# FFN standing tiles read with a step of two from interleaved storage, at sixteen places by piece

## The chip, the cores and the metric

One core of a Trainium2 chip. The metric is the device time of one execution in microseconds; the runs shown are executions of the same program.

## The reference, cut to what matters

Two blocks of two layers each over 256 rows of 1024 features. Every layer is an FFN, a mixer and another FFN, so there are eight FFNs; each is

```python
def swiglu(h, w_gate, w_up, w_down):
    a = jnp.einsum('bsd,df->bsf', h, w_gate)          # 1024 -> 2816
    u = jnp.einsum('bsd,df->bsf', h, w_up)
    return jnp.einsum('bsf,fd->bsd', jax.nn.silu(a) * u, w_down)   # 2816 -> 1024
```

in fp32. The mixers (attention of several kinds, a state-space scan, gated branches) are not touched by the change.

## The kernel before

**Products in halves.** Each fp32 operand is held as two fp32r tensors, `hi` and `lo`, whose sum it is, and each product is made of three: hi by hi, lo by hi and hi by lo. ScalarE writes `whi` from the loaded weights (`hi`, L1781), VectorE subtracts to get `wlo` (`lo`, L2038), in a few places GpSimd does (L2496).

**Pieces.** `plan()` cuts all weights into pieces of at most 1024 columns by 128 partitions in the order of their use; blocks of two pieces (1024 KB) are loaded by SyncE's queue into three `raw` buffers. A piece goes to `whi[i % 5]` and `wlo[i % 5]`, buffers of 1088 elements (4352 B, 17 x 256 B). `PLACES[i]` gives the element at which it starts there: 16 for the FFN's chunks 1 to 20 and some pieces of the mixers, 0 otherwise. The activations `xT` and `hT` start at the same point of 256 B as `wlo[0]` (`lined`).

**FFN.** `ffn` first makes the hidden features, 128 at a time. Chunk 0 goes through `gemm` and `rows`. Chunks 1 to 20 go through `gemm_w` and `columns` (L1589): the weight tile of 128 gate or up columns stands in TensorE, the 256 columns of `xT` move. A piece has four k-tiles of 128 gate and 128 up columns, so 4 x 2 x 3 = 24 matmuls; a chunk has two pieces, 48 matmuls, and its result is gate and up, one 256-column half of a PSUM bank each. ScalarE and VectorE turn it into `h` and then into the two halves of `hT` (`halve_h`, L1837 and L2130; for chunk 0, after a transpose, `turn_h`, L1810 and L2069).

The second gemm (`down`) goes through `rows` (L1570): a 128-column tile of `hT`, for row half t = 0 or 1, stands, and 512 weight columns move. 22 pieces of one k-tile with 2 x 2 x 3 = 12 matmuls, so 264.

Each matmul loads its own standing tile, and the load for the next one runs beside the current one. TensorE executes its queue in order. Between the FFN's up and down parts nothing stalls; `take` keeps `whi` and `wlo` up to five pieces ahead, and a piece's buffer comes free when the piece five before it is used (`hi` waits for `mm`).

Of the kernel before, what the change touches and what calls it, by code (L numbers as in the profile page):

```python
# [9 lines left out]
F32 = mybir.dt.float32  # L10
F32R = mybir.dt.float32r
ACT = mybir.ActivationFunctionType
# [82 lines left out]
QK1 = [[(n, c, c + 128) for n, c in _Q[4 * i:4 * i + 4]] for i in range(5)]  # L95

COLS = {}


def cols_plan():  # L100
# [69 lines left out]
class Signals:  # L170
    def __init__(self, sems):
        self.sems, self.value, self.sure = sems, {}, False
        self.n = {k: 0 for k in sems}
# [54 lines left out]
class Halves:  # L228


    def __init__(self, name, hi, lo, nk, both=None):
        self.name, self.H, self.L, self.both, self.gen = name, hi, lo, both, 0
        self.ready = [[None, None] for _ in range(nk)]
        self.free = ()


class Job:
# [17 lines left out]
    return 0, 0  # L255


PLACES = [place(key) for key, _, _ in plan()]


def upper(m, i):
# [9 lines left out]
def memory(nc, ctx):  # L271

    m = {}

    def sbuf(name, shape, dt=F32, scope=ctx):
        m[name] = scope.enter_context(nc.sbuf_tensor(name, shape, dt))
        return m[name]

    def lined(name, scope=ctx):

        rest = (at_line - nc.sbuf_base) % LINE // 32 * 32
        if rest:
            scope.enter_context(nc.sbuf_tensor(name + "_rest", [128, rest // 4], F32))

    def halves(name, nk, scope=ctx):
        lined(name, scope)
        m[name] = Halves(name, sbuf(name + "_hi", [128, nk, 256], F32R, scope),
                         sbuf(name + "_lo", [128, nk, 256], F32R, scope), nk)

    def many(name, n, shape, dt=F32, scope=ctx):  # L290
        m[name] = [sbuf(f"{name}{i}", shape, dt, scope) for i in range(n)]

    m["ps"] = [ctx.enter_context(nc.psum_tensor(f"ps{i}", [128, 512], F32)) for i in range(8)]
    many("raw", NRAW, [128, BLOCK])
    many("whi", NHL, [128, PIECE + SLACK], F32R)
    at_line = nc.sbuf_base % LINE
    many("wlo", NHL, [128, PIECE + SLACK], F32R)
    many("x", 2, [128, D])
    sbuf("xn", [128, 2, D])
    sbuf("ident", [128, 128])  # L300
    sbuf("cols", [128, NCOLS])
    sbuf("stat", [128, 512])
    sbuf("phalf", [128, 2])
    lined("xT")
    both = sbuf("xT_both", [128, 2, 8, 256], F32R)
    m["xT"] = Halves("xT", both[:, 0, :, :], both[:, 1, :, :], 8, both)

    def ffn(block):
        with ExitStack() as ph:
            halves("hT" + block, 22, ph)  # L310
            many("h" + block, 3, [128, 2, 256], F32, ph)
            sbuf("row" + block, [128, 256], F32, ph)

    with ExitStack() as b1:
        sbuf("rope1", [128, 2, 64], F32, b1)
        sbuf("causal", [128, 384], F32, b1)
        sbuf("dist", [128, 4, 384], F32, b1)
        ffn("1")
        with ExitStack() as ph:
            sbuf("qk1", [128, 18, 256], F32, ph)  # L320
            sbuf("v1", [128, 2, 1152], F32, ph)
            sbuf("o_dil3", [128, 2, 768], F32, ph)
            sbuf("o_dil", [128, 2, 256], F32, ph)
            halves("oTa", 3, ph)
            halves("oTb", 3, ph)
            many("sm1_", 2, [128, 384], F32, ph)
            many("pr1_", 3, [128, 384], F32, ph)
            many("pt1_", 2, [128, 384], F32, ph)
            with ExitStack() as pm:
                sbuf("lat", [128, 2, 416], F32, pm)  # L330
                sbuf("q_mla", [128, 2, 576], F32, pm)
                sbuf("k_mla", [128, 2, 576], F32, pm)
                sbuf("v_mla", [128, 2, 384], F32, pm)
                halves("cq", 2, pm)
                halves("ckv", 1, pm)
                sbuf("rope_a", [128, 2, 96], F32, pm)
                sbuf("rope_b", [128, 2, 96], F32, pm)
                many("qkT", 2, [96, 512], F32, pm)
            sbuf("g1", [128, 2, 3072], F32, ph)
    many("vr", 2, [128, D])  # L340
    sbuf("strict", [128, 384])
    sbuf("chunk", [128, 384])
    sbuf("rope2", [128, 2, 32])
    sbuf("ends", [128, 384])
    ffn("2")
    with ExitStack() as ph:
        sbuf("oa", [128, 2, 1024], F32, ph)
        sbuf("ob", [128, 2, 1024], F32, ph)
        many("sm2_", 2, [128, 385], F32, ph)
        many("pr2_", 3, [128, 384], F32, ph)  # L350
        many("pt2_", 2, [128, 384], F32, ph)
        sbuf("rw", [128, 272], F32, ph)
        sbuf("g2", [128, 6144], F32, ph)
        with ExitStack() as reg2:
            sbuf("bc", [128, 4, 256], F32, reg2)
            sbuf("xd", [128, 2, 1024], F32, reg2)
            many("sums", 2, [128, 4, 256], F32, reg2)
            many("decay", 2, [128, 4, 384], F32, reg2)
            sbuf("cb", [128, 2, 384], F32, reg2)
            many("conv", 3, [128, 256], F32, reg2)  # L360
            many("rot", 2, [128, 512], F32, reg2)
            many("rot_t", 2, [128, 128], F32, reg2)
            sbuf("dt8", [128, 8, 16], F32, reg2)
        sbuf("qkc", [128, 16, 256], F32, ph)
        sbuf("vc", [128, 2, 1024], F32, ph)
        halves("oT2", 8, ph)
    return m
# [1185 lines left out]
def tensor_program(engine, sg, m, steps, *_):  # L1553
    pe, e, at, mark = Lane(engine), engine, sg.at, sg.mark
    pieces, ident = plan(), m["ident"]

    def rows(i, t, job, lo_there, ready, banks):
        _, w, kts = pieces[i]
        hi, lo = upper(m, i), lower(m, i)
        pe.wait_ge(*at("hi", i))  # L1560
        for f in job.free[t]:
            pe.wait_ge(*at(*f))
        sl = slice(128 * t, 128 * t + 128)
        for n, (xs, ws) in enumerate(((job.H, hi), (job.L, hi), (job.H, lo))):
            if n == 2:
                pe.wait_ge(*at(*lo_there))
            for j, (_, kt, _) in enumerate(kts):
                pe.wait_ge(*at(*ready[j]))
                for bank, c0, c1 in [job.outs[t][b] for b in banks if b < len(job.outs[t])]:
                    made = e.matmul(bank[:, 0:c1 - c0], xs[:, kt, sl], ws[:, j * w + c0:j * w + c1],  # L1570
                                    start=kt == 0 and n == 0, stop=kt == job.nk - 1 and n == 2)
        made.then_inc(*mark("mm", i, t, *(banks if banks == (0,) else ())))

    def columns(i, job, lo_there, ready):
        _, w, kts = pieces[i]
        hi, lo = upper(m, i), lower(m, i)
        pe.wait_ge(*at("hi", i))
        for freed in job.free:
            for f in freed:
                pe.wait_ge(*at(*f))  # L1580
        for n, (ws, xs) in enumerate(((hi, job.H), (hi, job.L), (lo, job.H))):
            if n == 2:
                pe.wait_ge(*at(*lo_there))
            for j, (_, kt, _) in enumerate(kts):
                for there in ready[j]:
                    pe.wait_ge(*at(*there))
                for c, out in enumerate(job.outs):
                    o = j * w + 128 * c
                    made = e.matmul(out, ws[:, o:o + 128], xs[:, kt, :], start=kt == 0 and n == 0 and c % 2 == 0,  # L1589
                                    stop=kt == job.nk - 1 and n == 2, skip_group_check=True)  # L1590
        made.then_inc(*mark("mm", i, 1))

# [175 lines left out]
def scalar_program(engine, sg, m, steps, dram):  # L1768
# [38 lines left out]

    def turn_h(s, c, h, ps, free, hT):
        act.wait_ge(*at("tr", "h", s, c))
        e.activation(hT.H[:, 2 * c:2 * c + 2, :].rearrange("p a b -> p (a b)"), ps[:, :], ACT.Copy  # L1810
                     ).then_inc(*mark("xhi", "h", s, c))

    def halve_o(key, src, there, xt, k, n, xfree):
        act.wait_ge(*at(*there))
# [19 lines left out]

    def halve_h(s, c, h, hT):
        act.wait_ge(*at("gated", s, c, 0))
        e.activation(hT.H[:, c + 1, :], h[:, 0, :], ACT.Copy).then_inc(*mark("xhi", "h", s, c))  # L1837

    def mean_square(en, t, halves, rows, xn_free, ss, ms, r):
        for f in xn_free:  # L1840
# [182 lines left out]
def vector_program(engine, sg, m, steps, *_):  # L2023
# [41 lines left out]

    def turn_h(s, c, h, ps, free, hT):
        dve.wait_ge(*at("xhi", "h", s, c))
        hi = hT.H[:, 2 * c:2 * c + 2, :].rearrange("p a b -> p (a b)")
        e.tensor_tensor(hT.L[:, 2 * c:2 * c + 2, :].rearrange("p a b -> p (a b)"), ps[:, :], hi.bitcast(F32), sub  # L2069
                        ).then_inc(*mark("xlo", "h", s, c))  # L2070

    def mean_square(en, t, halves, rows, xn_free, ss, ms, r):
        dve.wait_ge(*at("sumsq", en, t))
# [53 lines left out]

    def halve_h(s, c, h, hT):
        dve.wait_ge(*at("xhi", "h", s, c))
        e.tensor_tensor(hT.L[:, c + 1, :], h[:, 0, :], hT.H[:, c + 1, :].bitcast(F32), sub  # L2130
                        ).then_inc(*mark("xlo", "h", s, c))

    def halve_o(key, src, there, xt, k, n, xfree):
# [489 lines left out]
```

## Time and profile before

| | us |
|---|---|
| median of 2 runs (2783.07 to 2783.18) | 2783.12 |
| the profiled execution | 2783.81 |
| its span, first to last instruction | 2782.0 |
| TensorE busy in it | 2761.5 |

The page gives the busy time of each engine, slices of the span, the chain of work that ended last and the costliest groups. Matmuls are pipelined, and a matmul's duration in the trace is longer than its distance to the next; for the pace of TensorE one divides the length of a stretch of back-to-back matmuls by their number. PE is the matmul side of TensorE, PEld its weight loads.

### The profile page before, as it was taken

The numbers are of one execution on the slowest core, as the hardware profiler recorded it, in microseconds if no ns is written. First come the engines' busy times: TensorE is split into PE (matmuls) and PEld (weight loads), VectorE is DVE, ScalarE is ACT, GpSimd is POOL, SyncE is SP. The second block draws the span as 40 slices with busy tenths as digits, with TensorE's granted clock in tenths as the row PEclk, the third lists the DMA queues.
The fourth block names the chain that finished last, engine by engine and source line by source line (L and its number), as shares of the span: only waits on it lengthen the run. The fifth ranks groups of instructions, "written<-read, shape, count | busy, mean of one in ns | idle before, by whom it ended". The sixth has DMA issues, their size and how long they took to land.

```text
span 2782.0 us, 44672 instructions
## 1 busy us (share of the span) xinstructions
PE 2761.5 (99%) x18116; PEld 2471.4 (89%) x18116; DVE 1822.0 (65%) x2860; ACT 1464.6 (53%) x2398; POOL 239.3 (9%) x187
## 2 busy tenths in 40 slices
PE   9999999999999999999999999999999999999998
PEld 8989889989989889989888987899899888878997
DVE  6656676646656666656568777765565687787755
ACT  6445555545455655444456566445454566655452
POOL 0010011010010010010014100110100131001100
PEclk9999999999999999999999999999999999999999
DMA  6544445555544345555555444555555554445653
GB/s 247 197 168 163 149 156 191 190 188 192 202 171 149 139 172 205 202 185 203 195 189 182 139 171 153 212 197 197 191 201 191 182 188 152 160 159 184 217 193 125
DMA packets 75068, 504.09 MB, mean 181 GB/s; under 512 B 8784, under 2 KB 10480, under 8 KB 19184
## 3 DMA queue, kind: packets, MB, share of 16 engines
q1 hardware_dynamic: 74576, 501.07, 50.7%
q8 instruction: 144, 2.36, 0.3%
q14 instruction: 60, 0.49, 0.1%
q10 hardware_dynamic: 288, 0.17, 0.0%
HBM read 500.12 MB, written 1.08 MB: 180 GB/s over the span
## 4 chain that ended last, share of the span: by engine, by line
PE 92%; DVE 5%; POOL 2%; ACT 1%; issue 1%; DMA 0%; SPq 0%; DVEq 0%; ACTq 0%
PE ps L1570 45%; PE ps L1589 39%; PE ps L1610 3%; POOL wlo L2496 2%; DVE wlo L2038 1%; DVE conv L2325 1%; PE ps L1705 1%; PE ps L1703 1%; PE ps L1730 1%; ACT whi L1781 0%; ACT conv L1949 0%; PE ps L1720 0%; PE ps L1721 0%; PE ps L1722 0%; DVE ps L2142 0%
## 5 line engine op out<-in xcount | busy, mean ns | idle before, releaser
L1781 ACT ACTIVATE whi<-raw 128x1024 fp32r<-128x1024 f32 (+3 forms) x938 | 975.9, 1043 | 636.8 <-PE ps L1570 428.8
L2038 DVE TENSOR_TENSOR wlo<-raw,whi 128x1024 fp32r<-128x1024 f32 (+2 forms) x894 | 1083.8, 1219 | 257.5 <-ACT whi L1781 256.5
L1589 PE MATMUL ps<-xT_both,whi 128*128 128x256 f32 x6592 | 824.2, 278 | 1.0 <-DVE v_mla L2252 1.0
L1589 PEld LDWEIGHTS ps<-xT_both,whi 128*128 128x128 f32 x6592 | 783.1, 188 | 8.3 <-issue 6.9
L1570 PE MATMUL ps<-whi,xT_both 128*128 128x512 f32 (+2 forms) x2336 | 628.6, 391 | 2.9 <-DVE xT_both L2061 1.6
L1570 PEld LDWEIGHTS ps<-whi,xT_both 128*128 128x128 f32 x2336 | 425.3, 188 | 84.2 <-issue 9.3
L1589 PE MATMUL ps<-xT_both,wlo 128*128 128x256 f32 x3296 | 442.5, 277 | 0.0
L1589 PEld LDWEIGHTS ps<-xT_both,wlo 128*128 128x128 f32 x3296 | 405.8, 188 | 0.0
L1570 PE MATMUL ps<-wlo,xT_both 128*128 128x512 f32 (+2 forms) x1168 | 354.4, 384 | 0.3 <-DVE wlo L2038 0.3
L1570 PEld LDWEIGHTS ps<-wlo,xT_both 128*128 128x128 f32 x1168 | 218.3, 188 | 43.7 <-DVE wlo L2038 1.4
L1570 PE MATMUL ps<-whi,hT_hi 128*128 128x512 f32 x704 | 221.4, 390 | 0.0
L1570 PE MATMUL ps<-whi,hT_lo 128*128 128x512 f32 x704 | 220.7, 389 | 0.0
L1570 PE MATMUL ps<-wlo,hT_hi 128*128 128x512 f32 x704 | 220.7, 389 | 0.0
L2496 POOL TENSOR_TENSOR wlo<-raw,whi 128x1024 fp32r<-128x1024 f32 (+1 forms) x44 | 102.5, 2348 | 1274.9 <-ACT whi L1781 1272.9
L2130 DVE TENSOR_TENSOR hT_lo<-h,hT_hi 128x256 fp32r<-128x256 f32 x160 | 68.1, 426 | 197.3 <-ACT hT_hi L1837 197.3
L1570 PEld LDWEIGHTS ps<-wlo,hT_hi 128*128 128x128 f32 x704 | 132.2, 188 | 27.5
L1570 PEld LDWEIGHTS ps<-whi,hT_lo 128*128 128x128 f32 x704 | 132.2, 188 | 27.3
L1570 PEld LDWEIGHTS ps<-whi,hT_hi 128*128 128x128 f32 x704 | 131.6, 188 | 26.6
L1833 ACT ACTIVATE h<-h 128x256 f32<-128x256 f32 x80 | 33.5, 419 | 141.0 <-DVE h L2121 141.0
L1871 ACT ACTIVATE pt<-ps 128x384 f32<-128x384 f32 x96 | 47.1, 491 | 91.8 <-PE ps L1610 90.9
L1830 ACT ACTIVATE h<-ps 128x256 f32<-128x256 f32 x80 | 30.7, 384 | 100.7 <-PE ps L1589 100.7
L2121 DVE TENSOR_TENSOR h<-ps,row 128x256 f32<-128x256 f32 x80 | 33.9, 424 | 68.1 <-PE ps L1589 68.1
(310 smaller groups left out, 2210.9 us busy)
## 6 DMA issues: line engine op xcount, KB each, us to landing
raw<-in_w SPq DMA_DIRECT2D x435, 1024.0 KB, 4.8
vr<-in_vrows SPq DMA_DIRECT2D x19, 512.0 KB, 6.1
raw<-in_w SPq DMA_DIRECT2D x12, 768.0 KB, 4.3
raw<-in_w SPq DMA_DIRECT2D x10, 896.0 KB, 4.5
sums<-scratch SPq DMA_DIRECT2D x8, 512.0 KB, 4.5
raw<-in_w SPq DMA_DIRECT2D x4, 832.0 KB, 4.5
raw<-in_w SPq DMA_DIRECT2D x4, 576.0 KB, 3.7
raw<-in_w SPq DMA_DIRECT2D x4, 512.0 KB, 6.9
```

Of the source, the lines that this page charges most:

```text
L1570: made = e.matmul(bank[:, 0:c1 - c0], xs[:, kt, sl], ws[:, j * w + c0:j * w + c1], start=kt == 0 and n == 0, stop=kt == job.nk - 1 and n == 2)
L1589: made = e.matmul(out, ws[:, o:o + 128], xs[:, kt, :], start=kt == 0 and n == 0 and c % 2 == 0, stop=kt == job.nk - 1 and n == 2, skip_gro ...
L1610: return e.transpose(out, in_, ident[0:k, 0:k])
L1703: e.matmul(ps[:, 0:128], qT[:, 0:128], kT[:, 0:128], start=True, stop=True)
L1781: e.activation(out, raw, ACT.Copy).then_inc(*mark("hi", i))
L1830: e.activation(h[:, 0, :], bank[:, 0:256], ACT.Silu).then_inc(*mark("silu", s, c, 0))
L1833: e.activation(h[:, 0, :], h[:, 0, :], ACT.Silu).then_inc(*mark("silu", s, c, 0))
L1871: e.activation(q[:, :], ps[:, 0:384], ACT.Copy).then_inc(*mark("pT", *key))
L2038: e.tensor_tensor(out, raw, hi.bitcast(F32), sub).then_inc(*mark("lo", i))
L2121: e.tensor_tensor(h[:, 0, :], bank[:, 0:256], row[:, :], mul).then_inc(*mark("scaled", "gate", s, c))
L2130: e.tensor_tensor(hT.L[:, c + 1, :], h[:, 0, :], hT.H[:, c + 1, :].bitcast(F32), sub).then_inc(*mark("xlo", "h", s, c))
L2496: e.tensor_tensor(out, raw, hi.bitcast(F32), ALU.subtract).then_inc(*mark("lo_p", i))
```

## The change

A chunk's piece, for chunks 1 to 20, is stored interleaved: column x of the gate tile at element 2x, column x of the up tile at 2x + 1 (the host writes the weights so). `columns` reads each standing tile with a step of two. In the same way `hT` holds row half t at elements 2x + t, `rows` reads its standing tile with a step of two, and the instructions that write `hT` write with that step; in `turn_h` there are two of them on each engine for one before. The start of these pieces, and of the second gemm's, within their buffers goes through sixteen values, 4 x (5i mod 16) elements for piece i, in place of 16 and 0. What is computed, the number of matmuls, loads and bytes, the order and the waits stay.

```diff
--- before.py
+++ after.py
@@ -97,6 +97,11 @@
+def woven(key):
+
+    return key[1] == "up" and key[3] > 0
+
+
 def cols_plan():
     out, at = [], 0
     for l in (0, 1):
@@ -228,10 +233,20 @@
 class Halves:
 
 
-    def __init__(self, name, hi, lo, nk, both=None):
+    def __init__(self, name, hi, lo, nk, both=None, woven=False):
         self.name, self.H, self.L, self.both, self.gen = name, hi, lo, both, 0
+        self.woven = woven
         self.ready = [[None, None] for _ in range(nk)]
         self.free = ()
+
+
+def by_tile(a):
+    return a.rearrange("p (t x) -> p t x", t=2)
+
+
+def tiles_of(a):
+
+    return a.rearrange("p (x t) -> p t x", t=2)
 
 
 class Job:
@@ -255,7 +270,8 @@
     return 0, 0
 
 
-PLACES = [place(key) for key, _, _ in plan()]
+PLACES = [(4 * (5 * i % 16),) * 2 if key[1] == "down" or woven(key) else place(key)
+          for i, (key, _, _) in enumerate(plan())]
 
 
 def upper(m, i):
@@ -282,10 +298,10 @@
         if rest:
             scope.enter_context(nc.sbuf_tensor(name + "_rest", [128, rest // 4], F32))
 
-    def halves(name, nk, scope=ctx):
+    def halves(name, nk, scope=ctx, woven=False):
         lined(name, scope)
         m[name] = Halves(name, sbuf(name + "_hi", [128, nk, 256], F32R, scope),
-                         sbuf(name + "_lo", [128, nk, 256], F32R, scope), nk)
+                         sbuf(name + "_lo", [128, nk, 256], F32R, scope), nk, woven=woven)
 
     def many(name, n, shape, dt=F32, scope=ctx):
         m[name] = [sbuf(f"{name}{i}", shape, dt, scope) for i in range(n)]
@@ -307,7 +323,7 @@
 
     def ffn(block):
         with ExitStack() as ph:
-            halves("hT" + block, 22, ph)
+            halves("hT" + block, 22, ph, True)
             many("h" + block, 3, [128, 2, 256], F32, ph)
             sbuf("row" + block, [128, 256], F32, ph)
 
@@ -1560,7 +1576,7 @@
         pe.wait_ge(*at("hi", i))
         for f in job.free[t]:
             pe.wait_ge(*at(*f))
-        sl = slice(128 * t, 128 * t + 128)
+        sl = slice(t, t + 255, 2) if job.xt.woven else slice(128 * t, 128 * t + 128)
         for n, (xs, ws) in enumerate(((job.H, hi), (job.L, hi), (job.H, lo))):
             if n == 2:
                 pe.wait_ge(*at(*lo_there))
@@ -1572,7 +1588,7 @@
         made.then_inc(*mark("mm", i, t, *(banks if banks == (0,) else ())))
 
     def columns(i, job, lo_there, ready):
-        _, w, kts = pieces[i]
+        key, w, kts = pieces[i]
         hi, lo = upper(m, i), lower(m, i)
         pe.wait_ge(*at("hi", i))
         for freed in job.free:
@@ -1585,8 +1601,8 @@
                 for there in ready[j]:
                     pe.wait_ge(*at(*there))
                 for c, out in enumerate(job.outs):
-                    o = j * w + 128 * c
-                    made = e.matmul(out, ws[:, o:o + 128], xs[:, kt, :], start=kt == 0 and n == 0 and c % 2 == 0,
+                    tile = slice(j * w + c, j * w + c + 255, 2) if woven(key) else slice(j * w + 128 * c, j * w + 128 * c + 128)
+                    made = e.matmul(out, ws[:, tile], xs[:, kt, :], start=kt == 0 and n == 0 and c % 2 == 0,
                                     stop=kt == job.nk - 1 and n == 2, skip_group_check=True)
         made.then_inc(*mark("mm", i, 1))
 
@@ -1807,8 +1823,9 @@
 
     def turn_h(s, c, h, ps, free, hT):
         act.wait_ge(*at("tr", "h", s, c))
-        e.activation(hT.H[:, 2 * c:2 * c + 2, :].rearrange("p a b -> p (a b)"), ps[:, :], ACT.Copy
-                     ).then_inc(*mark("xhi", "h", s, c))
+        for j in (0, 1):
+            made = e.activation(tiles_of(hT.H[:, 2 * c + j, :]), by_tile(ps[:, 256 * j:256 * j + 256]), ACT.Copy)
+        made.then_inc(*mark("xhi", "h", s, c))
 
     def halve_o(key, src, there, xt, k, n, xfree):
         act.wait_ge(*at(*there))
@@ -1834,7 +1851,7 @@
 
     def halve_h(s, c, h, hT):
         act.wait_ge(*at("gated", s, c, 0))
-        e.activation(hT.H[:, c + 1, :], h[:, 0, :], ACT.Copy).then_inc(*mark("xhi", "h", s, c))
+        e.activation(tiles_of(hT.H[:, c + 1, :]), by_tile(h[:, 0, :]), ACT.Copy).then_inc(*mark("xhi", "h", s, c))
 
     def mean_square(en, t, halves, rows, xn_free, ss, ms, r):
         for f in xn_free:
@@ -2065,9 +2082,10 @@
 
     def turn_h(s, c, h, ps, free, hT):
         dve.wait_ge(*at("xhi", "h", s, c))
-        hi = hT.H[:, 2 * c:2 * c + 2, :].rearrange("p a b -> p (a b)")
-        e.tensor_tensor(hT.L[:, 2 * c:2 * c + 2, :].rearrange("p a b -> p (a b)"), ps[:, :], hi.bitcast(F32), sub
-                        ).then_inc(*mark("xlo", "h", s, c))
+        for j in (0, 1):
+            made = e.tensor_tensor(tiles_of(hT.L[:, 2 * c + j, :]), by_tile(ps[:, 256 * j:256 * j + 256]),
+                                   tiles_of(hT.H[:, 2 * c + j, :]).bitcast(F32), sub)
+        made.then_inc(*mark("xlo", "h", s, c))
 
     def mean_square(en, t, halves, rows, xn_free, ss, ms, r):
         dve.wait_ge(*at("sumsq", en, t))
@@ -2127,7 +2145,7 @@
 
     def halve_h(s, c, h, hT):
         dve.wait_ge(*at("xhi", "h", s, c))
-        e.tensor_tensor(hT.L[:, c + 1, :], h[:, 0, :], hT.H[:, c + 1, :].bitcast(F32), sub
+        e.tensor_tensor(tiles_of(hT.L[:, c + 1, :]), by_tile(h[:, 0, :]), tiles_of(hT.H[:, c + 1, :]).bitcast(F32), sub
                         ).then_inc(*mark("xlo", "h", s, c))
 
     def halve_o(key, src, there, xt, k, n, xfree):
@@ -2590,11 +2608,15 @@
         dst = wpack[at:at + 128 * used].reshape(128, used)
         at += 128 * used
         for i, off, n in ps:
-            _, width, kts = pieces[i]
+            key, width, kts = pieces[i]
+            first = off
             for idx, kt, ranges in kts:
                 for name, c0, c1 in ranges:
                     dst[:, off:off + c1 - c0] = a[name][idx][128 * kt:128 * kt + 128, c0:c1]
                     off += c1 - c0
+            if woven(key):
+                pairs = dst[:, first:off].reshape(128, len(kts), 2, 128)
+                dst[:, first:off] = pairs.transpose(0, 1, 3, 2).reshape(128, -1)
     cols = _np.zeros((128, NCOLS), _np.float32)
     for name, l, c, n in _COLS:
         v = a[name][l]
```

## Rows read from the trace of the kernel before

**Rows 1.** The page's head: busy us (share of the span) and number of instructions.

```profile
span 2782.0 us, 44672 instructions
PE 2761.5 (99%) x18116; PEld 2471.4 (89%) x18116; DVE 1822.0 (65%) x2860; ACT 1464.6 (53%) x2398; POOL 239.3 (9%) x187
```

**Rows 2.** Groups by form, TensorE: shapes, count, busy us, mean ns, idle before.

```profile
L1589 PE MATMUL ps<-xT_both,whi 128*128 128x256 f32 x6592 | 824.2, 278 | 1.0 <-DVE v_mla L2252 1.0
...
L1589 PE MATMUL ps<-xT_both,wlo 128*128 128x256 f32 x3296 | 442.5, 277 | 0.0
L1570 PE MATMUL ps<-whi,hT_hi 128*128 128x512 f32 x704 | 221.4, 390 | 0.0
...
L1604 PE MATMUL ps<-xT_both,whi 128*16 128x256 f32 x32 | 5.7, 279 | 0.0
```

**Rows 3.** Chain of waits, first and last FFN: start us, us, what, count.

```profile
21.41 5.65 PE ps L1589 x48
...
27.95 103.38 PE ps L1589 x912
131.33 58.51 PE ps L1570 x258
...
2610.58 103.38 PE ps L1589 x912
2713.96 53.08 PE ps L1570 x234
```

**Rows 4.** Windows of the first FFN: length, busy us (count), granted clock, DMA share, GB/s.

```profile
27.80:131.10 103.30, 103.30 (x914) 103.30 (x913) 67.41 (x96) 52.69 (x78) 0.00 (x0) 1.00 0.58 205
131.20:189.60 58.40, 58.40 (x260) 48.34 (x259) 27.01 (x28) 23.75 (x27) 2.76 (x3) 1.00 0.50 176
```

**Rows 5.** Timeline of matmuls with 384 moving columns: start us, us, what.

```profile
264.32 0.85 PE L1570 MATMUL ps<-whi,xT_both 128*128 128x384 f32 x4
265.01 0.51 PE L1570 MATMUL ps<-wlo,xT_both 128*128 128x384 f32 x2
265.36 0.85 PE L1570 MATMUL ps<-whi,xT_both 128*128 128x384 f32 x4
```

**Rows 6.** Timeline of weight loads in a run of transposes.

```profile
1694.87 1.56 PEld L1610 LDWEIGHTS ps<-ident,ob 128*128 128x128 f32 x14
1696.40 0.75 PEld L1570 LDWEIGHTS ps<-whi,xT_both 128*128 128x128 f32 x4
```

**Rows 7.** Chain of waits in the first mixer: the chunks' form at two levels.

```profile
218.04 11.54 PE ps L1589 x96
...
239.42 5.66 PE ps L1589 x48
```

**Rows 8.** Timeline of weight loads before chunk 2: a standing tile read without a step.

```profile
27.23 0.53 PEld L1652 LDWEIGHTS ps<-ident,stat 128*128 128x128 f32 x4
27.68 0.65 PEld L1589 LDWEIGHTS ps<-xT_both,whi 128*128 128x128 f32 x5
```

**Rows 9.** Chain of waits: 24 matmuls of L1604, a 16-column standing tile.

```profile
1434.99 2.81 PE ps L1604 x24
```

**Rows 10.** Groups by form in 27.80 to 131.10: the writers of hT.

```profile
L2130 DVE TENSOR_TENSOR hT_lo<-h,hT_hi 128x256 fp32r<-128x256 f32 x19 | 8.1, 426 | 18.8 <-ACT hT_hi L1837 18.8
...
L1837 ACT ACTIVATE hT_hi<-h 128x256 fp32r<-128x256 f32 x19 | 7.6, 400 | 0.0
L2069 DVE TENSOR_TENSOR hT_lo<-ps,hT_hi 128x512 fp32r<-128x512 f32 x1 | 0.7, 692 | 1.2 <-ACT hT_hi L1810 1.2
L1810 ACT ACTIVATE hT_hi<-ps 128x512 fp32r<-128x512 f32 x1 | 0.6, 598 | 1.2 <-PE ps L1610 1.2
```

**Rows 11.** DMA issues in 27.80 to 189.00: count, KB each, median us to landing.

```profile
raw<-in_w SPq DMA_DIRECT2D x27, 1024.0 KB, 4.8
```


## The prediction

> **What bounds the kernel.** I read the page first. TensorE is busy for 2761.5 us of a span of 2782.0 us, VectorE for 65% and ScalarE for 53% [rows 1]. A busy TensorE is not yet a TensorE at its peak, so the next question is how long it takes for one matmul. The groups by form give the counts: 9888 products with a weight chunk standing and 256 columns of activations moving (L1589), and 3 x 704 = 2112 products of the FFN's second gemm, hT standing and 512 weight columns moving (L1570) [rows 2]. Their mean durations (277 and 389 ns) overlap; the chain of waits gives the true pace, since it merges back-to-back matmuls into one piece with a count. In the first FFN, 912 chunk matmuls take 103.38 us, 113.4 ns each, and 258 of the second gemm take 58.51 us, 226.8 ns each; the last FFN shows the same [rows 3]. The 48 of chunk 1 run at 5.65 / 48 = 117.7 ns. The windows show TensorE busy in every microsecond of both stretches at a granted clock of 1.00, its higher level (2.4 GHz), while VectorE has a third of the first stretch free and ScalarE half [rows 4]. So in the FFNs, which the change touches, the pace of TensorE alone sets the time; every nanosecond off a matmul comes off the end.
>
> Matmuls touched: 8 FFNs x 20 chunks x 48 = 7680 chunk matmuls (7296 at 113.4 ns, 384 at 117.7) and 2112 second-gemm matmuls at 226.8 ns. That is 827.4 + 45.2 + 479.0 = 1351.6 us, almost half of the span. Only they can move.
>
> **What a matmul's time is made of.** Six matmuls of 384 columns take 265.36 - 264.32 = 1.04 us, 173.3 ns each [rows 5]; 512 columns take 226.8. So 128 more columns cost 53.5 ns, 0.418 ns each: one column per cycle of 2.4 GHz. Then 512 columns stream in 213.3 ns and 13.5 ns are excess; 256 stream in 106.7 ns and the excess is 6.7 ns, or 11.0 in chunk 1. The other limit is the weight load, of which there is one for each matmul: in transposes, whose 128 moving columns would need only 53 ns, 14 loads take 1696.40 - 1694.87 = 1.53 us, 109.3 ns each [rows 6], 0.854 ns per standing column. So a chunk matmul has two nearly equal limits, 106.7 and 109.3 ns, and takes 113.4.
>
> Where does the excess come from? Not from the other engines: in the first 912 matmuls ScalarE and VectorE start and stop some 170 times, and the mean is 113.4 ns at both ends of the kernel [rows 3, 4]. But the same form takes 113.4 ns in one stretch and 117.7 or 120.2 ns in another [rows 3, 7], with the same operands and no idle time inside. So part of the excess depends on how the two reads of TensorE itself, the moving tile and the next standing tile, stand to each other. With a step of one the moving read advances 4 B per 0.418 ns (9.6 B/ns) and the standing read 4 B per 0.854 ns (4.7 B/ns): one overtakes the other through whatever banks the storage has, again and again. With a step of two the standing read advances 8 B per 0.854 ns, 9.4 B/ns: the two run side by side and hardly overtake. That is the mechanism I take as likeliest.
>
> **The change, part by part.**
>
> *Chunk matmuls (standing tile read with a step of two).* If the overtaking is the excess, what remains is the load's 109.3 ns: 7296 x (113.4 - 109.3) = 29.9 us and 384 x (117.7 - 109.3) = 3.2 us, together -33 us. Bounds: no change gives 0; a load cannot come under 109.3 by any row, so -33 is also the end of the gain. On the other side a strided load may be dearer. The one standing tile of this trace that is not read contiguously (a step of zero, L1652) takes 27.68 - 27.23 = 0.45 us for four, 112.5 ns [rows 8]; that is the nearest row, and at 112.5 ns the gain shrinks to 7296 x 0.9 + 384 x 5.2 = 8.6 us. I take 109.3, since a step of zero hits one spot of the storage and a step of two does not.
>
> The Trainium skill, "SBUF — State Buffer", Specifications, says storage is read by 16-byte lines that want at least two hits each for full bandwidth. A step of two in fp32 has exactly two hits per line, so by that page the strided load keeps its pace; a step of four would not. No row of the trace of before shows a step of two.
>
> *Second gemm (hT standing with a step of two, weights moving from sixteen places).* The load fits twice into the matmul, so only the stream and its excess count. The smallest excess of any row is 6.7 ns [rows 3]; at 213.3 + 6.7 = 220.0 the gain is 2112 x 6.8 = 14.4 us. Ends: none, and the whole excess, 2112 x 13.5 = 28.5 us. One row speaks for a floor under the excess: with a standing tile of only 16 columns, where hardly any load runs beside the stream, 256 columns still take 2.81 / 24 = 117 ns [rows 2, 9]. I take 14.4.
>
> The Trainium skill, "TensorE: Matmul & The Clock Gate", Back-to-back issue gap, gives N/2.4 + 2.5 ns. By that page 512 columns would take 215.8 ns, and the second term would be 2112 x 11.0 = 23 us instead of 14.4.
>
> *Places.* A piece starts at 4 x (5i mod 16) elements, 16 B steps over 256 B; hT and xT stay where they were. One piece in sixteen has both reads start at the same place. There I price a collision as the slow rows do: a chunk matmul at 117.7 rather than 109.3, 480 x 8.4 = 4.0 us; a second-gemm matmul at 226.8 rather than 220.0, 132 x 6.8 = 0.9 us. So +5 us.
>
> *ScalarE and VectorE.* The two halves of an hT tile are now written with a step of two (L1837, L2130: 400 and 426 ns), and the first tile's halves in two instructions rather than one (598 and 692 ns, once per FFN) [rows 10]. If the strided writes took double, each engine would carry 0.4 us more for each chunk of 5.4 us; VectorE is busy for 67.41 of 103.30 us there. Hidden, zero. Without that cover it would be 160 x 0.4 = 64 us, but nothing in TensorE's queue waits for an hT tile until the second gemm, up to twenty chunks later. Transfers: a block of 1024 KB lands in 4.8 us [rows 11]; two pieces would take 2 x 24 x 0.1093 = 5.25 us, and three blocks are in flight or in use. Hidden, though with less room than before (5.44 us). The host's reordering of the weights costs the device nothing, and bytes and packets are the same.
>
> Sum: -33 - 14 + 5 = -42 us. The profiled execution took 2783.8 us (its span 2782.0 and 1.8 around it), 0.7 above the median; the difference holds for both, so 2783.1 - 42 = **2741 us**, or -1.5%.
>
> **The rivals.**
>
> *Faster still.* All excess of the second gemm goes and no place collides: -33 - 28.5 = -61.6 us, 2721.5. For it: the excess of 13.5 ns is twice that of the chunks, so it is not one constant. Against it: the 16-column row.
>
> *The excess is not made by the two reads* (the change doesn't do what it says). Then it is fixed per matmul and only the 384 slow ones might move: 2780 to 2783. For it: the 16-column row again, and excesses that are the same to 0.1 ns in all eight FFNs. The Trainium skill, "SBUF — State Buffer", Who interferes with whom, says TensorE has two independent read ports and never waits for anyone; by that page this rival is right. The two levels of the same form [rows 3, 7] speak against it.
>
> *Side by side is worse.* Reads that advance at one pace stay wherever they begin; if they begin in a collision they may keep it. If most places behave as the slow rows, 7296 x 4.3 = 31 us and, at the same share (4%) for the second gemm, 19 us are added: 2833.
>
> *The strided load is slow.* This one decides for slower. A chunk matmul has only 113.4 - 109.3 = 4.1 ns of room above its load. With the second gemm's gain of 14 us kept, the kernel is slower as soon as a load with a step of two takes over 113.4 + 1.9 = 115.3 ns, 5% more than a contiguous one; by over 2% from 122.6 ns. At one and a half times the contiguous load, 164 ns, it is 7680 x 50 = +390 us, 3160 us; at twice, +800. Nothing in the trace excludes it, as no row reads so; what speaks against it is that the moving stream takes 9.6 B/ns and a strided load asks for 9.4.
>
> **How the numbers follow.** I give 0.52 to the forecast with its own range 2728 to 2760; 0.08 to faster still; 0.16 to no change (2770 to 2785); 0.11 to side by side is worse (2785 to 2835); 0.13 to the slow load. A measurement of this kernel tells 2% from no change, 55.7 us: under 2727.5 is faster, over 2838.8 slower. Faster gets 0.07, slower 0.14, the same 0.79. The range from 2721 to 2815 holds the forecast, nearly all of faster still, no change and over half of the worse case: about 0.8.
>
> **What the profile after would show.** In the chain of waits the piece of 912 should shrink from 103.4 to about 100 us, and the 258 from 58.5 to about 56.8. Chunk 1 should lose its slow level. If the load is slow, the weight loads of L1589 will be longer than 188 ns and lie end to end. If the places decide, pieces of one FFN will differ with a period of sixteen, where now all are equal. VectorE's idle time before wlo should shrink a little. All else, the mixers above all, should keep its microseconds; if they move, I have missed a coupling.

## The result and the profile after

| | before | after |
|---|---|---|
| median, us | 2783.12 (2783.07 to 2783.18) | 2842.97 (2842.66 to 2843.29) |
| span of the profiled execution, us | 2782.0 | 2841.5 |
| TensorE busy, us | 2761.5 | 2820.5 |

The ratio is 1.0215, with a 95% interval of 1.0171 to 1.0259: 59.9 us slower, by the median a little over the 2% bound, which the interval includes. I had forecast 2741 us and a range up to 2815.

The page's head of the changed kernel (answers to [rows 1]): TensorE's busy time grew by 59.0 us, ScalarE's by 2.8 and VectorE's by 0.1.

```profile
span 2841.5 us, 44688 instructions
PE 2820.5 (99%) x18116; PEld 2534.1 (89%) x18116; DVE 1822.1 (64%) x2868; ACT 1467.4 (52%) x2406; POOL 239.5 (8%) x187
```

The chain of waits of the changed kernel, first and last FFN: start us, us, what, count (answers to [rows 3]).

```profile
22.02 5.74 PE ps L1605 x48
...
28.64 109.35 PE ps L1605 x912
...
137.99 59.88 PE ps L1586 x258
...
2662.82 109.35 PE ps L1605 x912
2772.17 54.31 PE ps L1586 x234
```

912 chunk matmuls take 109.35 us where they took 103.38: 119.9 ns each, not 113.4. 258 of the second gemm take 59.88 where they took 58.51: 232.1 ns, not 226.8. Over eight FFNs that is 8 x 5.97 = 47.8 us, and 2112 x 1.37 / 258 = 11.2 us; chunk 1 (5.74 for 5.65) gives 0.7. Together 59.7 us: the whole difference, and all of it in the matmuls that the change touches.

Groups by form of the changed kernel in 28.5 to 137.8, the first FFN's chunks (the writers of hT answer to [rows 10]), and below them the weight loads of the kernel before in 27.8 to 131.1:

```profile
L1605 PEld LDWEIGHTS ps<-xT_both,whi 128*128 128x128 f32 x608 | 75.7, 196 | 0.0
...
L2148 DVE TENSOR_TENSOR hT_lo<-h,hT_hi 128x256 fp32r<-128x256 f32 x19 | 8.1, 426 | 22.1 <-ACT hT_hi L1854 22.1
...
L1854 ACT ACTIVATE hT_hi<-h 128x256 fp32r<-128x256 f32 x19 | 8.0, 420 | 0.0
```

```profile
L1589 PEld LDWEIGHTS ps<-xT_both,whi 128*128 128x128 f32 x608 | 71.7, 188 | 0.0
```

The record of a weight load is 8 ns longer, as I had written for the slow load. By itself this sign proves little: in the first FFN of `places_even` below, where the tiles are contiguous and the matmuls also take 120.0 ns, the records of the loads are 192 ns. The strided writes cost nothing on VectorE (426 ns in both) and 20 ns on ScalarE, hidden.

### The profile page after: what moved, and what is told of

Same layout as the page of the kernel before. It is cut to its first block, busy times and chain, and to the rows that moved or that the text cites. A ratio compares the mean times of both kernels' runs of the same rounds, so it can differ in the third digit from the quotient of the medians.

```text
span 2841.5 us, 44688 instructions
## 1 busy us (share of the span) xinstructions
PE 2820.5 (99%) x18116; PEld 2534.1 (89%) x18116; DVE 1822.1 (64%) x2868; ACT 1467.4 (52%) x2406; POOL 239.5 (8%) x187
## 4 chain that ended last, share of the span: by engine, by line
PE 92%; DVE 4%; POOL 2%; ACT 1%; issue 1%; DMA 0%; SPq 0%; DVEq 0%; ACTq 0%
PE ps L1586 44%; PE ps L1605 40%; PE ps L1626 3%; POOL wlo L2514 2%; DVE wlo L2055 1%; DVE conv L2343 1%; PE ps L1721 1%; PE ps L1719 1%; PE ps L1746 1%; ACT whi L1797 0%; ACT conv L1966 0%; PE ps L1736 0%; PE ps L1737 0%; DVE ps L2160 0%; PE ps L1738 0%
## 5 line engine op out<-in xcount | busy, mean ns | idle before, releaser
L1605 PE MATMUL ps<-xT_both,whi 128*128 128x256 f32 x6592 | 856.0, 283 | 1.0 <-DVE v_mla L2270 1.0
L1605 PEld LDWEIGHTS ps<-xT_both,whi 128*128 128x128 f32 x6592 | 815.1, 194 | 8.3 <-issue 6.9
L1605 PE MATMUL ps<-xT_both,wlo 128*128 128x256 f32 x3296 | 458.6, 282 | 0.0
L1605 PEld LDWEIGHTS ps<-xT_both,wlo 128*128 128x128 f32 x3296 | 422.6, 194 | 0.0
```

The lines of the kernel that those rows point to most:

```text
L1605: made = e.matmul(out, ws[:, tile], xs[:, kt, :], start=kt == 0 and n == 0 and c % 2 == 0, stop=kt == job.nk - 1 and n == 2, skip_group_ch ...
```

## The experiments

### Step or places?

`places_only` is the kernel before with the sixteen places, `step_only` the changed kernel with the places of before.

```diff
-PLACES = [place(key) for key, _, _ in plan()]
+PLACES = [(4 * (5 * i % 16),) * 2 if key[1] == "down" or (key[1] == "up" and key[3] > 0) else place(key)
+          for i, (key, _, _) in enumerate(plan())]
```

```diff
-PLACES = [(4 * (5 * i % 16),) * 2 if key[1] == "down" or woven(key) else place(key)
-          for i, (key, _, _) in enumerate(plan())]
+PLACES = [place(key) for key, _, _ in plan()]
```

> The kernel before, contiguous, with the sixteen places alone (chunks 1 to 20 and the second gemm). Three theories. (1) A load with a step of two is slow by itself: the places matter little, 912 chunk matmuls stay near 103.4 us, total near 2783. (2) The two reads of TensorE disturb each other, more when they advance at one pace: contiguous reads overtake each other at any place, so the pieces differ by place between 113.3 and 118 ns and the total is 2785 to 2815. (3) The places alone did it and the step is innocent: 912 chunk matmuls take about 109.4 us, 258 of the second gemm 59.9, total about 2843.

> The changed kernel with its pieces at the places of before (16 and 0), so the step of two alone. Theory 1 (slow load): chunk matmuls at about 120 ns whatever the place, the second gemm little changed, 2830 to 2840. Theory 2 (the reads disturb each other at one pace): the changed kernel's own pieces at these places took 119.9 ns and 233.2 ns, so 912 take 109.4 us, 258 take 60.1 us, total about 2844. Theory 3 (places): 2783.

Measured: 2831.36 us for the places alone (ratio 1.017, 1.0153 to 1.0187), 2846.18 for the step alone (1.0224, 1.0209 to 1.024); the kernel before beside them 2783.64. Chain of waits, `places_only` and then `step_only`:

```profile
28.49 107.78 PE ps L1590 x912
136.28 59.96 PE ps L1571 x258
```

```profile
28.24 109.45 PE ps L1604 x912
137.69 60.20 PE ps L1585 x258
```

Each of the two edits is slow by itself (47.7 us, just under 2%, and 62.5 us), and they don't add: with the step, the places give back 3 us. The contiguous places cost more than any of my theories had for them but the third, which the second run refutes.

### What does a load cost by itself?

The first try cut the moving side of the chunks to 64 columns (`cut = 64`, in `out` and `xs`), contiguous and with the step.

> The kernel before, in which the chunk matmuls after the first of a bank move 64 columns rather than 256, so most of the product is left out; the loads are all there and set the pace. All theories: a contiguous load alone takes 109.3 ns, as in transposes, so 912 take about 100 us (the 38 full ones 113), total about 2753.

> The changed kernel with the same cut: 64 moving columns in the chunk matmuls after the first of a bank (most of the product left out), loads with a step of two. Theory 1 (slow load): 912 matmuls stay at about 109 us (120 ns each), total about 2842. Theory 2 (the reads disturb each other) and theory 3: the load alone is as fast as a contiguous one, 912 in about 100 us, and the total is that of the same cut without the step plus some 11 us from the second gemm, about 2765.

Measured: 3525 and 3549 us. The windows (length, busy us (count), granted clock, DMA share, GB/s), contiguous and then with the step:

```profile
28.20:222.50 194.30, 194.30 (x913) 194.30 (x912) 67.08 (x96) 52.17 (x77) 0.00 (x0) 0.50 0.31 109
```

```profile
30.10:224.40 194.30, 194.30 (x913) 194.30 (x913) 67.14 (x97) 52.51 (x77) 0.00 (x0) 0.50 0.31 109
```

Expected were 2753 us for the first and 2765 or 2842 for the second, all at the higher clock, and neither came: TensorE was granted 0.50, its lower level of 1.2 GHz. There a load takes 213 ns with either step, so a step of two is free at half the clock; for the full clock the pair says nothing.

So `steps` narrows only every fourth piece, and tries more steps in one kernel. `cut` is 128 in the second piece of even chunks, `cols` 16 in that of odd ones:

```diff
+                        step = (1, 2, 3, 4, 8)[(key[3] - 1) // 4]
+                        if step > 1:
+                            first = (2 * j + c) % step
+                            tile = slice(first, first + 127 * step + 1, step)
...
+                    made = e.matmul(out[0:cols, 0:cut], ws[:, tile][:, 0:cols], xs[:, kt, 0:cut],
```

> The kernel before, in which chunks 1 to 4 read their standing tile with a step of 1, 5 to 8 with 2, 9 to 12 with 3, 13 to 16 with 4 and 17 to 20 with 8, from the storage as it is (so the product is not the reference's from chunk 5 on). In even chunks the second piece moves 128 columns rather than 256, which leaves the load alone to set the pace; in odd chunks the second piece has standing tiles of 16 columns rather than 128, which leaves the stream alone (both leave work out). Theory 1 (a load with a step of two is slow by itself): load alone 109.3 ns at a step of 1 and about 120 at 2. Theory 2 (the two reads disturb each other): load alone 109.3 at both, whole matmuls 113.4 at 1 and 120.0 at 2. The Trainium skill, SBUF — State Buffer, Specifications, wants two hits on each 16-byte line: by it the load alone would become dearer from a step of 3 on. Both theories: the stream beside a 16-column load takes 107 to 117 ns.

Measured: 3172.41 us. The granted clock was 0.955 in the mean, but it fell to its lower level in stretches of 3.4 to 10.2 us, most of them among the chunks with steps of three and more. Of the pairs below, the first four lie wholly at the higher level; the last (step of eight) was at the lower one from 154.80 on. Timeline of weight loads in `steps` (start us, us, what), second pieces of chunks 4, 8, 10, 14 and 18, that is steps of 1, 2, 3, 4 and 8; the distance of the two starts in a pair is 16 loads:

```profile
41.75 1.86 PEld L1599 LDWEIGHTS ps<-xT_both,whi 128*128 128x128 f32 x16
43.54 0.97 PEld L1599 LDWEIGHTS ps<-xT_both,wlo 128*128 128x128 f32 x8
...
64.44 1.99 PEld L1599 LDWEIGHTS ps<-xT_both,whi 128*128 128x128 f32 x16
66.35 1.04 PEld L1599 LDWEIGHTS ps<-xT_both,wlo 128*128 128x128 f32 x8
...
78.45 2.90 PEld L1599 LDWEIGHTS ps<-xT_both,whi 128*128 128x128 f32 x16
81.26 1.49 PEld L1599 LDWEIGHTS ps<-xT_both,wlo 128*128 128x128 f32 x8
...
112.81 3.83 PEld L1599 LDWEIGHTS ps<-xT_both,whi 128*128 128x128 f32 x16
116.55 1.96 PEld L1599 LDWEIGHTS ps<-xT_both,wlo 128*128 128x128 f32 x8
...
152.50 3.96 PEld L1599 LDWEIGHTS ps<-xT_both,whi 128*128 128x128 f32 x16
156.36 2.01 PEld L1599 LDWEIGHTS ps<-xT_both,wlo 128*128 128x128 f32 x8
```

| step | 16-byte lines in a load | load beside 128 columns, ns | ns per line |
|---|---|---|---|
| 1 | 32 | 1.79 / 16 = 112 | 3.5 |
| 2 | 64 | 1.91 / 16 = 119 | 1.87 |
| 3 | 96 | 2.81 / 16 = 176 | 1.83 |
| 4 | 128 | 3.74 / 16 = 234 | 1.83 |
| 8 | 128 | 3.86 / 16 = 241 | 1.88 |

One more piece with a step of four, the second of chunk 16, ran into such a stretch. Below are its loads and two windows: one inside the piece of chunk 14, one inside this one (last columns: granted clock, DMA share, GB/s).

```profile
132.47 3.83 PEld L1599 LDWEIGHTS ps<-xT_both,whi 128*128 128x128 f32 x16
136.21 1.96 PEld L1599 LDWEIGHTS ps<-xT_both,wlo 128*128 128x128 f32 x8
```

```profile
112.90:117.20 4.30, 4.30 (x20) 4.30 (x20) 0.42 (x1) 1.37 (x2) 0.00 (x0) 1.00 0.09 36
134.40:137.90 3.50, 3.50 (x16) 3.50 (x17) 0.23 (x1) 0.00 (x0) 0.00 (x0) 0.50 0.02 5
```

Its 16 loads take the same 3.74 us, and those that lie in the stretch at 0.50 are 233 ns apart, as at 1.00. The price of a line does not follow TensorE's clock, while that of a column does: a contiguous load took 112 ns at the higher level and 213 at the lower. So at 1.2 GHz the columns hide the lines of a step of two (64 x 1.87 = 120 ns), but not those of a step of four.

This settles the first question: a load with a step of two is slow by itself, with 53 ns of stream beside it. From a step of two on, it costs 1.83 to 1.88 ns for each 16-byte line that it touches; a contiguous load touches few lines and is limited by its 128 columns instead. The Trainium skill, "SBUF — State Buffer", Specifications, gives the right quantity, lines, but its two hits per line are not quite enough here: at two, the lines take 119 ns and the columns 112.

### Which standing tile?

`weights_only` and `ht_only` have the step for one kind of tile, at the places of before. In the first hT is written and read contiguously. In the second the chunk weights are stored as before, and:

```diff
-                    tile = slice(j * w + c, j * w + c + 255, 2) if woven(key) else slice(j * w + 128 * c, j * w + 128 * c + 128)
+                    tile = slice(j * w + 128 * c, j * w + 128 * c + 128)
```

> The step of two for the chunk weights alone, at the places of before; hT contiguous as before. New theory 4 (each 16-byte line that a read touches costs TensorE some 1.8 ns, so a load with a step of two, 64 lines, is limited to 120 ns by itself; a longer stream beside it is slowed by its additional lines): 912 chunk matmuls take 109.4 us, the second gemm goes back to 58.5 us for 258 (226.8 ns), total about 2832. If the second gemm's level of 233.3 ns came from how it is entered, out of slow chunks, and not from its own step: 258 in 60.2 us, total about 2846.

> The step of two for hT alone, at the places of before; chunk weights contiguous. Theory 4: chunks at 103.4 us for 912 as before, second gemm at 60.2 us for 258 (233.3 ns), total 2783 + 2112 x 6.5 ns = 2797. If the second gemm's level comes from how it is entered: 58.5 us and 2783.

Measured, once each: 2832.38 and 2797.11 us, beside 2783.07 (seven executions of the kernel before, beside the first pair, lay between 2782.81 and 2784.42). Chain of waits, `weights_only` and then `ht_only`:

```profile
27.76 109.44 PE ps L1604 x912
137.20 58.52 PE ps L1585 x258
```

```profile
27.82 103.38 PE ps L1604 x912
131.19 60.20 PE ps L1585 x258
```

Each tile's step costs its own matmuls, 49.3 and 14.0 us, and leaves the others as they were; 63.3 together, where the step alone cost 62.5. The second gemm of `weights_only` comes out of slow chunks and is fast.

### Lines or columns, and the stream

`lines` and `streams` alter the same pieces in other ways, for instance these (the rest of the edit is left out):

```diff
+                            if g == 1:
+                                moving = moving.rearrange("p (a b) -> p a b", b=8)[:, :, 0:4]
+                            if g == 2:
+                                moving = moving.rearrange("p (a b) -> p a b", b=4)[:, :, 0:2]
```

> The kernel before, with the second piece of chunks 1 to 20 altered and most of its work left out (not the reference's product). Even chunks, load of 128 columns beside a short stream: chunks 2 and 4 contiguous beside 128 moving columns, 6 and 8 the same from 2 elements later (33 lines rather than 32), 10 and 12 contiguous beside 64, 14 and 16 with a step of two beside 64, 18 and 20 contiguous beside 192. Odd chunks, stream beside a load of 16 columns: 1 and 3 256 columns contiguous (64 lines), 5 and 7 128 columns as 4 of each 8 (32 lines), 9 and 11 128 as 2 of each 4 (64 lines), 13 and 15 128 with a step of two (64 lines), 17 and 19 64 with a step of four (64 lines). Theory 4 (a line costs 1.8 ns): odd chunks 113 to 117 ns for each with 64 lines, 56 to 60 with 32 lines; even chunks 109 to 113 ns contiguous, 120 with the step of two whatever the stream. If columns count and not lines: 113, 56, 56, 56, 28 to 50 ns in the odd chunks. If the 120 ns of a load with a step of two come from the stream beside it, they fall towards 109 beside 64 columns.

> The kernel before with chunks altered once more (most of the work left out, not the reference's product). Odd chunks of all FFNs, second piece, stream beside a load of 16 columns: 1 and 3 192 columns contiguous (48 lines), 5 and 7 128 with a step of four (128 lines), 9 and 11 128 with a step of three (96 lines), 13 and 15 192 as 4 of each 8 (48 lines), 17 and 19 128 with a step of eight (128 lines). If each line costs a stream 1.8 ns: 86, 233, 175, 86, 233 ns. If a column costs 0.44 ns where lines are read whole and 0.9 ns where they are not (the 60 ns for 64 columns with a step of four speak for this): 85, 116, 116, 85, 116. Even chunks of the first four FFNs, contiguous load begun 0, 8, 16, 28 and 44 elements later for the five groups of four chunks, whole matmuls in the first piece and 128 moving columns in the second: if the place acts through the two reads together, the first pieces take 113.4, 117 to 119, 118.7, 118, 120 ns and the second 111.7 throughout. Even chunks of the last four FFNs, second piece, load beside a short stream: 64 standing columns contiguous, with a step of four (64 lines), of eight (64 lines), of two (32 lines), each beside 64 columns, and 128 with a step of two beside 192. If each line costs a load 1.83 ns: 60 (the least that any matmul takes here), 117, 120, 60, 120.

Measured: 2761.53 and 2767.51 us, with much of the work left out, so only the stretches count. Timeline of matmuls in `lines`: chunk 3 (256 columns contiguous beside a 16-column load), chunk 13 (128 columns with a step of two) and chunk 17 (64 with a step of four).

```profile
36.33 1.98 PE L1611 MATMUL ps<-xT_both,whi 128*16 128x256 f32 x16
38.15 1.07 PE L1611 MATMUL ps<-xT_both,wlo 128*16 128x256 f32 x8
...
88.47 2.03 PE L1611 MATMUL ps<-xT_both,whi 128*16 128x128 f32 x16
90.30 0.43 PE L1611 MATMUL ps<-xT_both,wlo 128*16 128x128 f32 x2
...
110.84 1.12 PE L1611 MATMUL ps<-xT_both,whi 128*16 128x64 f32 x16
111.79 0.66 PE L1611 MATMUL ps<-xT_both,wlo 128*16 128x64 f32 x8
```

Timeline of matmuls in `streams`: chunks 4 and 6 of the sixth FFN (64 standing columns contiguous, 16 lines, and with a step of four, 64 lines), and chunk 5 of the second (128 moving columns with a step of four).

```profile
1840.50 1.07 PE L1612 MATMUL ps<-xT_both,whi 128*64 128x64 f32 x16
1841.41 0.63 PE L1612 MATMUL ps<-xT_both,wlo 128*64 128x64 f32 x8
...
1852.19 1.12 PE L1612 MATMUL ps<-xT_both,wlo 128*64 128x64 f32 x8
1853.15 0.36 PE L1612 MATMUL ps<-xT_both,whi 128*128 128x256 f32 x1
...
473.68 1.12 PE L1612 MATMUL ps<-xT_both,wlo 128*16 128x128 f32 x8
474.62 0.66 PE L1612 MATMUL ps<-xT_both,whi 128*128 128x256 f32 x4
```

*Loads: lines.* 64 standing columns take (1841.41 - 1840.50) / 16 = 57 ns contiguous and (1853.15 - 1852.19) / 8 = 120 ns with a step of four, as much as 128 columns with a step of two. Both touch 64 lines. With a step of two, 32 lines, the 64 columns take 58 ns, and with a step of eight, again 64 lines, 121. And 128 with a step of two stay at 118 ns beside 64 moving columns and beside 192, so the stream is not the cause.

*Streams: not lines.* Beside a 16-column load, 256 contiguous columns take (38.15 - 36.33) / 16 = 114 ns, 128 with a step of two (90.30 - 88.47) / 16 = 114, and 128 with a step of four (474.62 - 473.68) / 8 = 118. Here twice the lines cost 4 ns and not another 117; 64 columns with a step of four touch 64 lines in 60 ns. A stream takes some 0.45 ns for a column where it uses each line that it touches whole (also when every other line is left out, 87 ns for 192 columns as 4 of each 8) and about 0.9 ns where it uses only a part of them. My line price failed for the moving side (233 ns expected, 118 measured).

*The excess of 6.7 ns.* A stream of 256 columns has it with almost no load beside it, so these 6.7 ns do not come from two reads overtaking each other, as I had believed. What comes on top can appear there too: in chunk 1 of `lines` the same 256 columns beside a contiguous 16-column load take 118 ns.

### Places

`places_odd` and `places_even` are contiguous with one place for each FFN; `step_best` is the changed kernel with all pieces at the two places where its own were fastest.

```diff
+FFN_PLACE = dict(zip((("f1", 0), ("f2", 0), ("f1", 1), ("f2", 1), ("F1", 0), ("F2", 0), ("F1", 1), ("F2", 1)),
+                     (0, 8, 16, 24, 32, 40, 48, 56)))
```

```diff
+PLACES = [(60, 60) if key[1] == "down" else (20, 20) if woven(key) else place(key) for key, _, _ in plan()]
```

> The kernel before, contiguous, with one fixed place for each FFN: 4, 12, 20, 28, 36, 44, 52 and 60 elements for FFN 1 to 8, chunks 1 to 20 and second gemm alike. Theory 2, in the form that the place of a contiguous tile alone sets the excess: the chunk levels repeat those of the rotated kernel, 118.8, 118.3, 118.7, 119.6, 119.4, 118.5, 116.7, 119.4 ns; the second gemm 231.6, 232.8, 231.3, 226.6, 233.1, 232.6, 234.1, 233.6. If instead mixing places is what disturbs, all are near 113.4 and 226.8.

> The same with 0, 8, 16, 24, 32, 40, 48 and 56 elements for FFN 1 to 8. By the place alone: chunks 119.8, 118.2, 113.4, 117.9, 119.0, 119.9, 118.0, 117.0 ns; second gemm 226.8 at 0 (as in the kernel before), then 233.1, 230.5, 234.2, 231.4, 234.1, 232.5, 233.4. If mixing places is what disturbs, all are near 113.4 and 226.8.

> The changed kernel with all chunk pieces at element 20 and all of the second gemm at 60, the places at which its own pieces were fastest (117.8 and 229.5 ns). If the place alone decides: 912 in 107.5 us, 258 in about 59, total about 2820. If at one fixed place the two reads settle in a common level, as with 16 and 0: 120.0 and 233.3 ns, total about 2845.

Measured, once each: 2835.71, 2827.87 and 2845.92 us, beside 2783.81. Chain of waits of `places_even`, FFNs at 0, 16 and 40, and of `step_best`:

```profile
28.47 109.43 PE ps L1592 x912
137.89 58.51 PE ps L1573 x258
...
649.82 103.39 PE ps L1592 x912
753.21 59.06 PE ps L1573 x258
...
1863.46 109.44 PE ps L1592 x912
1972.90 54.82 PE ps L1573 x234
```

```profile
28.56 109.44 PE ps L1604 x912
138.01 60.21 PE ps L1585 x258
```

For contiguous chunk tiles, place 16 alone gives 113.4 ns; the fifteen others lie between 116.7 (52 and 56) and 120.0 (0, 28, 36, 40 and 60). The second gemm has 226.8 ns at 0 and 28 and 228.9 to 236.7 elsewhere. So the kernel before sat at the one good place of sixteen for the chunks and at one of two for the second gemm. In `streams` a contiguous load begun 8 to 44 elements later is in its whole matmuls at 118 to 120 ns, while the same load beside 128 moving columns stays at 112 at each place: the place acts through the load and a full stream together. Only the weights' place was moved in any run, never that of xT or hT, so that it is the place of one read relative to the other is my reading and not shown.

With the step, 16 and 20 both give 120.0 ns and 0 and 60 give 233.3 and 233.4 ns, once all pieces have one place. The changed kernel's own pieces do differ, with a period of sixteen as I had named it. Timeline of weight loads of the changed kernel, pieces at 0, 20 and 40 elements:

```profile
57.23 2.00 PEld L1605 LDWEIGHTS ps<-xT_both,whi 128*128 128x128 f32 x16
...
60.11 1.96 PEld L1605 LDWEIGHTS ps<-xT_both,whi 128*128 128x128 f32 x16
...
62.94 2.00 PEld L1605 LDWEIGHTS ps<-xT_both,whi 128*128 128x128 f32 x16
```

The piece at 20 takes 62.94 - 60.11 = 2.83 us, 118 ns for a matmul, that at 0 takes 2.88. But with all at 20 it is 120.0. Part of the level is thus carried from what ran before and not fixed by the place; chunk 1 of the kernel before, at 117.7 ns where the others have 113.4 at the same place, is another case of it [rows 3]. So are 96 matmuls of the first mixer, which the change doesn't touch: 11.54 us before [rows 7], and in the changed kernel

```profile
226.06 11.14 PE ps L1605 x96
```

## Why the prediction was wrong, point by point

- *What sets the time* held: TensorE's pace alone, in the FFNs alone. 59.7 of the 59.9 us are there, and no other engine or transfer took part. The mixers keep theirs but for tenths (11.14 for 11.54 us in the 96 matmuls above).
- *The chunk matmuls* are the step that failed. I let the strided load keep the contiguous 109.3 ns, as it asks for no more bytes per ns than the stream gets. It is limited by the lines it touches, 64 rather than 32, at 1.83 to 1.88 ns each: 117 to 120 ns. The term was not -33 us but +49.3 (`weights_only`). The row I had set beside it, the step of zero at 112.5 ns [rows 8], touches one line over and over and could say nothing of this. Nor was there anything to gain: a contiguous load of weights beside a short stream takes 112 ns and not the 109.3 of the transposes, and 256 moving columns take 113.4 ns even beside a 16-column load (114 in the pair above), so by these rows the stream would have kept the piece of 912 at 103.4 us whatever the load did.
- *The rival "the strided load is slow"* is what happened. Its point of decision, 115.3 ns, held, and so did its arithmetic: 7680 x (120.0 - 113.6) = 49 us. I had priced it at half as much again and at twice, and not at the 10% in between, and gave it 0.13; it also kept the second gemm's gain, which did not come. With a price for a line it would have led.
- *The overtaking of two reads* as the source of the excess is refuted by the stream beside a 16-column load. The row that spoke against it stood in the prediction [rows 9], and I used it for the second gemm's floor and between the rivals, but not against the gain of the chunks. That the place of a contiguous load moves the level shows the load and the stream acting on each other; what they do to each other is open. The two levels at one place [rows 3, 7], which I had taken as the sign of it, were no proof, as they stand beside a 16-column load too (114 and 118 ns in `lines`). The rival that the two reads do not make the excess was thus right for the 6.7 ns, and its time of 2780 to 2783 us was wrong.
- *The second gemm* is the other step that failed. It has 226.8 ns for a load of 120, and still lost 6.5 ns per matmul: +14.0 us (`ht_only`), where I had -14.4. That additional lines of the load hold up the stream would fit; it was not shown, and no run here varies the lines alone at 512 columns with all else kept. The nearest pieces don't decide it: in `steps` 256 columns beside a 16-column load take (38.24 - 36.42) / 16 = 114 ns contiguous and (49.29 - 47.43) / 16 = 116 with a step of two, but `lines` has 118 with a contiguous one.
- *Places*: +5 us in the sum, in truth -3 beside the step. Alone they cost 47.7 us. I had priced one place in sixteen as bad, while fifteen of sixteen are bad for contiguous chunk tiles; the kernel before did not show that, as it has no chunk at another place.
- *Side by side is worse* had 2833 us, near the result, by the wrong mechanism: beside a short stream the strided load is as slow.
- *ScalarE, VectorE, transfers*: zero, as written.

## What to carry to other kernels

Where the standing tile's load and the moving stream are nearly equal, price the load by the larger of its columns (0.87 ns each at 2.4 GHz, 1.67 at 1.2) and its 16-byte lines (1.83 to 1.88 ns each at either): for fp32r at 2.4 GHz, a step of two already crosses over. And treat the place of the standing or the moving weights as a parameter that is worth measuring over its whole range, alone, before other edits are laid over it: here it is worth 6.6 ns in 113, as much as the step. At the lower clock a step of two was free, so a test that leaves TensorE at 1.2 GHz hides it; what the place does there was not measured with whole matmuls.

## What the runs showed of the hardware that I had not expected

A load with a step of four costs 234 ns, at either level of the clock, and with a step of eight 241, twice the contiguous stream of 256 columns beside it. A moving read is not priced so: 128 moving columns with a step of two, three, four or eight take 110 to 118 ns, while 128 as 4 of each 8 take 60, which is near the least that any piece of these products took (64 standing columns beside 64 moving, 57 ns). Why a step of eight is a little cheaper there than one of four is open, and so is what carries the level of one piece to the next.
